# Combining the experts' rows: seven token groups in 128 slots, tokens beyond them sent aside through memory

## What is computed

```python
g_sel = argmax(g_logits)                    # one group of 8 for each token
top_val, top_idx = top_k(e_in_group, 2)     # two experts of that group
y[token] = sum over the two: gate * ((silu(x @ w1[e]) * (x @ w3[e])) @ w2[e])
h = h + y
out = rmsnorm(h, final_norm)
```

## Time and profile before

| | us |
|---|---|
| median of 3 timed runs | 1466.49 (1465.53 to 1470.39) |
| the profiled execution | 1461.49 |
| its span, first to last instruction | 1459.8 |
| experts, first up projection to last combine | 939.4 to 1448.6 |

### The profile page before, as it was taken

How to read it: one execution, slowest core, us unless ns; L and a number is a source line. 1 busy time by engine, 2 the same in 40 slices (tenths; PEclk the granted TensorE clock), 3 DMA queues, 4 the chain that set the end, 5 groups by cost and what they waited for, 6 DMA issues and landing times. The chain is left out here.

```text
span 1459.8 us, 22021 instructions
## 1 busy us (share of the span) xinstructions
PE 1420.7 (97%) x8759; PEld 1013.9 (69%) x8759; DVE 780.8 (53%) x1703; ACT 515.7 (35%) x992; POOL 82.4 (6%) x115
## 2 busy tenths in 40 slices
PE   9999999999999999999989999899999999999995
PEld 8888887797878877677768888755545555545552
DVE  6455565433531154667758555555654655555553
ACT  6525354222332147555543456412121212212121
POOL 0000000000000000000000011200101101011000
PEclk9999999999999999999999999999999999999998
DMA  6111111112224335112236634899999999999940
GB/s 176 44 30 44 30 38 36 30 33 87 86 88 118 104 92 161 59 37 73 72 122 221 252 123 151 307 411 418 419 420 419 420 418 419 419 418 419 419 199 16
DMA packets 114680, 286.38 MB, mean 196 GB/s; under 512 B 28926, under 2 KB 75006, under 8 KB 90258
## 3 DMA queue, kind: packets, MB, share of 16 engines
q1 hardware_dynamic: 105362, 263.95, 48.4%
q0 software_dynamic: 9216, 21.02, 3.7%
HBM read 270.19 MB, written 23.10 MB: 201 GB/s over the span
## 5 line engine op out<-in xcount | busy, mean ns | idle before, releaser
L134 PE MATMUL ps<-uTh,h_wh 128*128 128x512 f32 (+2 forms) x672 | 255.5, 380 | 0.0
L136 PE MATMUL ps<-uTh,h_wl 128*128 128x512 f32 (+2 forms) x672 | 247.8, 369 | 0.0
L135 PE MATMUL ps<-uTl,h_wh 128*128 128x512 f32 (+2 forms) x672 | 247.7, 369 | 0.0
L2617 PE MATMUL ps<-r,m_xT 128*64 128x256 f32 x2048 | 246.2, 391 | 0.4 <-DVE m_xT L2412 0.4
L2617 PEld LDWEIGHTS ps<-r,m_xT 128*64 128x64 f32 x2048 | 141.4, 134 | 89.3 <-issue 13.7
L134 PEld LDWEIGHTS ps<-uTh,h_wh 128*128 128x128 f32 x672 | 126.3, 188 | 22.5 <-issue 0.4
L136 PEld LDWEIGHTS ps<-uTh,h_wl 128*128 128x128 f32 x672 | 126.3, 188 | 18.9
L135 PEld LDWEIGHTS ps<-uTl,h_wh 128*128 128x128 f32 x672 | 126.5, 188 | 18.3 <-issue 0.2
L589 DVE TENSOR_TENSOR h_wl<-h_w,h_wh 128x1024 fp32r<-128x1024 f32 (+1 forms) x42 | 50.6, 1204 | 157.0 <-ACT h_wh L402 156.9
L2582 PE MATMUL ps<-r,m_small 128*64 128x512 f32 x512 | 124.1, 605 | 1.6 <-DVE m_small L2486 0.9
L2333 ACT ACTIVATE m_small<-ps,scale 128x128 f32<-128x128 f32 x64 | 23.4, 366 | 266.9 <-PE ps L2617 266.9
(11 more groups left out here) (423 smaller groups left out, 2356.8 us busy)
## 6 DMA issues: line engine op xcount, KB each, us to landing
r<-in_w SPq DMA_DIRECT2D x190, 1024.0 KB, 15.8
h_w<-in_w_in SPq DMA_DIRECT2D x37, 512.0 KB, 4.2
gates<-h_sg POOLq DMA_DIRECT2D x16, 512.0 KB, 2.9
br_gate<-gates SPq DMA_DIRECT2D x14, 512.0 KB, 4.9
e_wo<-in_w_out SPq DMA_DIRECT2D x4, 1024.0 KB, 7.9
f_x<-in_x SPq DMA_DIRECT2D x8, 512.0 KB, 5.0
h_half<-f_half SPq DMA_DIRECT2D x8, 512.0 KB
gates<-br_gate SPq DMA_DIRECT2D x6, 512.0 KB, 2.7
```

The source lines that it names most:

```text
L134: pe.matmul(out, lh, rh, start=start, stop=False)
L135: pe.matmul(out, lh, rl, start=False, stop=False)
L136: return pe.matmul(out, ll, rh, start=False, stop=stop)
L2617: ins = pe.matmul(up_out(e, 0, DE, CAP * f, CAP * (f + 1)).rearrange("p (r f) -> p r f", r=2), xT[i % 2][:, j, CAP * k:CAP * (k + 1)], g.r ...
```

## The change

1. For seven groups the token list kept on the chip is its first 128. `combine` leaves out line 2595 for the first EDGE = 28 pairs; the last group (pairs 28 to 31) keeps `rest`, now in another buffer. `roots`, `sums` and `scaled` handle `o2` for the last group alone, with one instruction of 128 x 512 in place of two and gains of its own (`gain_half`).
2. `one_hot` writes its matrix with a row sum (`found`): 1 if the slot's token is among the 128, else 0. A further instruction of one column makes `aside` = 2 token + choice, plus 4096 where it was found, which is out of bounds. It runs at the start of the next even iteration, ahead of the hidden rows. `spread_rows` and `row` move an iteration forward.
3. POOL sends each of the 28 pairs aside with an indirect scatter of its 128 rows to `g.y` at `aside`: only rows of tokens beyond the 128 move. The gather into the same buffer waits for that scatter's landing and for the last `low` of the pair, in place of `combine`.
4. At the start of the experts, `past`, `past_ranks`, `past_spots`, `past_list` and `past_lists` number the tokens beyond and make a list of them. During the last group two gathers fetch their two rows, DVE adds, ACT and DVE normalise, and a third indirect DMA writes them out.
5. `g.y` is filled beforehand, 8 DMAs of 1 MB from memory to memory, one after each of the weight loads J = 2..9 on SP. The slot lists carry a fourth column block (the choice), from which `dstf` is made.
6. The repeat through `late_blocks` is now taken if the tokens beyond, summed over seven groups, exceed 128, or the last group exceeds 192. `lo` is one buffer of 128 x 512.

```diff
...
             for J in range(2, len(JOBS)):
                 sp.wait_ge(wl_ok, J - 1)
                 load_w(J)
+                if J < 10:
+                    n = J - 2
+                    sp.dma_start(g.y[n * 256:(n + 1) * 256, :], g.x[0, n % 4 * 256:(n % 4 + 1) * 256, :]).then_inc(y_filled, 16)
...
+            dve.wait_ge(rows_ok, 6)
+            for k, part in halves:
+                dve.scalar_tensor_tensor(out=g.dstf[part, :], in0=srcf[part, :], scalar=2.0,
+                                         in1=LISTS(3 * EXPERTS, EXPERTS)[part, k::2], op0=ALU.mult, op1=ALU.add).then_inc(rows_ok, 1)
...
-                pe.matmul(LISTS(0, 3 * EXPERTS), Pm[:, 1, :], V[t % 2][:, 1, 0:3, :].rearrange("p v e -> p (v e)"),
+                pe.matmul(LISTS(0, 4 * EXPERTS), Pm[:, 1, :], V[t % 2][:, 1, :, :].rearrange("p v e -> p (v e)"),
...
             def give(n):
                 pool.wait_ge(to_ok, 3)
-                pool.wait_ge(o_ok, 3 * n + 1)
...
-                pool.wait_ge(o_ok, 3 * n + 3)
-                settle(pool, g)
-                pool.indirect_dma_start(out=g.out[0].rearrange("t (c d) -> (t c) d", c=2),
-                                        out_offset=bass.IndirectOffsetOnAxis(ap=to_half[:, n:n + 1], axis=0),
-                                        in_=o2[:, :], in_offset=None, bounds_check=2 * SEQ - 1, oob_is_err=False).then_inc(o2_out, 16)
...
-            pool.memset(x[ROWBUF - 1], 0.0).then_inc(rows_zero, 1)
-            for n in range(XB - 1, PAIRS):
-                if n == ROWBUF - 1:
-                    pool.wait_ge(rows_zero, 1)
-                elif n >= ROWBUF:
-                    pool.wait_ge(cmb_mm, 2 * (n - ROWBUF) + 2)
-                if n >= 2 * PER and n % PER == 0:
-                    give(n // PER - 2)
...
+            def gather(n):
...
+            for i in range(EDGE):
+                pool.wait_ge(aside_ok, i + 1)
+                pool.wait_ge(y_ok, 4 * i + 4)
+                settle(pool, g)
+                pool.indirect_dma_start(out=g.y, out_offset=bass.IndirectOffsetOnAxis(ap=aside[:, i:i + 1], axis=0),
+                                        in_=x[i % ROWBUF], in_offset=None,
+                                        bounds_check=2 * SEQ - 1, oob_is_err=False).then_inc(aside_out, 16)
+                if i and i % PER == 0:
+                    give(i // PER - 1)
+                pool.wait_ge(aside_out, 16 * i + 16)
+                pool.wait_ge(lo_ok, 2 * i + 2)
+                gather(i + ROWBUF)
+            pool.wait_ge(dn_mm, EXPERTS - PER_GROUP + 2)
+            pool.wait_ge(beyond_ok, 3)
+            for r in range(2):
+                settle(pool, g)
+                pool.indirect_dma_start(out=left_y[:, r, :], out_offset=None, in_=g.y,
+                                        in_offset=bass.IndirectOffsetOnAxis(ap=aside_at[:, r:r + 1], axis=0),
+                                        bounds_check=2 * SEQ - 1, oob_is_err=False).then_inc(left_in, 16)
             give(GROUPS - 2)
+            pool.wait_ge(left_ok, 1)
+            settle(pool, g)
+            pool.indirect_dma_start(out=g.out[0], out_offset=bass.IndirectOffsetOnAxis(ap=aside_at[:, 2:3], axis=0),
+                                    in_=left_y[:, 0, :], in_offset=None, bounds_check=SEQ - 1, oob_is_err=False).then_inc(left_out, 16)
             give(GROUPS - 1)
...
-                if n:
-                    act.wait_ge(o2_out, 16 * n)
-                act.activation(o2[:, :], bank(MORE_BANK), ACT.Square, accum_out=st[:, 0:1]).then_inc(ss_ok, 1)
-                act.wait_ge(s2_ok, 2 * n + 2)
-                act.wait_ge(ss_ok, 2 * n + 2)
+                if n == GROUPS - 1:
+                    act.activation(o2, bank(MORE_BANK), ACT.Square, accum_out=st[:, 0:1]).then_inc(ss_ok, 1)
+                    act.wait_ge(s2_ok, 2)
+                act.wait_ge(ss_ok, n + 1)
...
+            def left_root():
+                act.wait_ge(left_sum, 1)
+                act.activation(left_y[:, 1, :], left_y[:, 0, :], ACT.Square, accum_out=st[:, 1:2]).then_inc(left_ss, 1)
+                act.wait_ge(left_ss, 1)
+                act.activation(st[:, 1:2], st[:, 1:2], ACT.Sqrt, scale=1.0 / D, bias=g.eps[:, :]).then_inc(left_rt, 1)
+                act.activation(warm[:, :], g.eps[:, :], ACT.Sigmoid)
...
+            def past_spots():
+                dve.wait_ge(beyond_mm, 1)
+                c.link(dve.tensor_copy(beyond_at, beyond_out))
+                for t in range(TT):
+                    dve.tensor_scalar(beyond_spot[t], g.io_group[:, 0:P], beyond_at[:, t:t + 1], beyond[:, t:t + 1], ALU.is_equal,
+                                      ALU.mult).then_inc(beyond_spot_ok, 1)
...
+            def left_added():
+                dve.wait_ge(left_in, 32)
+                dve.tensor_tensor(left_y[:, 0, :], left_y[:, 0, :], left_y[:, 1, :], ALU.add).then_inc(left_sum, 1)
...
+            def left_scaled():
+                dve.wait_ge(left_rt, 1)
+                dve.reciprocal(st[:, 1:2], st[:, 1:2]).then_inc(left_rc, 1)
+                dve.wait_ge(left_rc, 1)
+                dve.scalar_tensor_tensor(out=left_y[:, 0, :], in0=left_y[:, 0, :], scalar=st[:, 1:2], in1=gain, op0=ALU.mult,
+                                         op1=ALU.mult).then_inc(left_ok, 1)
...
             def one_hot(i):
                 dve.wait_ge(row_mm, i // PER + 1)
                 if i >= 2:
                     dve.wait_ge(cmb_mm, 2 * i - 2)
-                dve.tensor_scalar(hot[i % 2], row_out[:, 0:P], g.srcf[:, i:i + 1], None, ALU.is_equal).then_inc(hot_ok, 1)
-                dve.tensor_scalar(rest(i % 2, 64, 64), row_out[:, P:GC], g.srcf[:, i:i + 1], None, ALU.is_equal).then_inc(hot_ok, 1)
-
-            def sums(n):
-                dve.wait_ge(ss_ok, 2 * n + 2)
+                dve.scalar_tensor_tensor(out=hot[i % 2], in0=row_out[:, 0:P], scalar=g.srcf[:, i:i + 1], in1=g.ones[:, :],
+                                         op0=ALU.is_equal, op1=ALU.mult, accum_out=found[:, i % 2:i % 2 + 1]).then_inc(hot_ok, 1)
+                if i < EDGE:
+                    dve.wait_ge(hot_ok, hot_at(i))
+                    dve.scalar_tensor_tensor(out=aside[:, i:i + 1], in0=found[:, i % 2:i % 2 + 1], scalar=SKIP, in1=g.dstf[:, i:i + 1],
+                                             op0=ALU.mult, op1=ALU.add).then_inc(aside_ok, 1)
+                else:
+                    if i == EDGE:
+                        for b in range(3):
+                            dve.tensor_scalar(rest(b, 0, 64), g.ones[:, 0:64], 0.0, None, ALU.mult).then_inc(hot_ok, 1)
+                    dve.tensor_scalar(rest(i % 2, 64, 64), row_out[:, P:GC], g.srcf[:, i:i + 1], None, ALU.is_equal).then_inc(hot_ok, 1)
+
...
-                for q in range(2):
-                    rows = slice(64 * q, 64 * (q + 1))
-                    dve.scalar_tensor_tensor(out=o2[rows, :], in0=bank(MORE_BANK, 0, 512, 64 * q, 64 * (q + 1)), scalar=st[rows, 7:8],
-                                             in1=gain[rows, 512 * q:512 * (q + 1)], op0=ALU.mult, op1=ALU.mult).then_inc(o_ok, 1)
+                if n == GROUPS - 1:
+                    dve.wait_ge(gain_half_in, 32)
+                    dve.scalar_tensor_tensor(out=o2, in0=bank(MORE_BANK), scalar=st[:, 7:8], in1=gain_half, op0=ALU.mult,
+                                             op1=ALU.mult).then_inc(o_ok, 1)
...
-            for b in range(3):
-                dve.tensor_scalar(rest(b, 0, 64), g.ones[:, 0:64], 0.0, None, ALU.mult).then_inc(hot_ok, 1)
+            dve.tensor_scalar(st, g.ones[:, 0:8], 1.0, None, ALU.mult).then_inc(st_ok, 1)
...
+                if e % 2 == 0 and 4 <= e < EXPERTS - 2:
+                    one_hot(e // 2 - 1)
...
+                    past()
...
-                if e % PER_GROUP == 1:
-                    spread_rows(e // PER_GROUP)
+                    spread_rows(0)
+                if e == 2:
+                    past_spots()
                 if e % 2 == 0 and 2 <= e < EXPERTS - 2:
                     low(e // 2 - 1, 0)
-                    one_hot(e // 2 - 1)
-                if e % PER_GROUP == 1 and e > PER_GROUP:
-                    sums(e // PER_GROUP - 1)
+                if e == 2:
+                    one_hot(0)
+                if e == 3:
+                    past_lists()
+                if e % PER_GROUP == 0 and e:
+                    spread_rows(e // PER_GROUP)
+                if e == EXPERTS - 4:
+                    left_added()
+                if e == EXPERTS - 3:
+                    left_scaled()
...
+            def past_ranks():
+                pe.wait_ge(member_ok, 4)
+                pe.matmul(beyond_out, g.upper[:, :], beyond, start=True, stop=False)
+                for n in range(1, TT):
+                    ins = pe.matmul(beyond_out[:, n:TT], g.ones[:, :], beyond[:, 0:TT - n], start=False, stop=n == TT - 1)
+                ins.then_inc(beyond_mm, 1)
+
+            def past_list():
+                pe.wait_ge(beyond_spot_ok, TT)
```

(47 more changed lines are left out.)

85 lines of the change are left out of this document (61 added, 24 removed).

## The result

The changed kernel takes 1444.85 us (1440.82 to 1445.83, four runs) where the kernel before took 1466.01 (1461.87 to 1470.39, four runs on the same chip): a ratio of 0.985, 95% interval 0.9815 to 0.9885, a gain of 21.2 us. Forecast were 24 us and 1442.5. The profiled execution of after took 1445.61 us, its span is 1443.9.

The account below looks back on a forecast made before the run. PE was taken to set the pace, with DMA a second bound. PE's side, 26.3 + 9.9 - 4.5 = 31.7 us, is capped by DMA at 24.7; less up to 1, gain 24: 1466.5 - 24 = 1442.5 us, range 1434 to 1453.

Parts of the forecast that it names:

- The likeliest case: Whole kernel: PE gives up 31.7 us, DMA allows 24.7, the smaller counts; gain 21 to 27 us, chance 0.58.
- (a): Combines of the first 28 pairs: 112 places lose PE matmuls at 0.235 us each, saving 26.3 us.
- part is given back: Rival: second combines wait for `high` and `low`, so 13.2 us are lost; 1448, or 1455 with DVE's instructions; chance 0.18.
- (b): Turn of each group: PE's waits for one-hots (8.5 us) and transposed rows (1.4) go, saving 9.9 us.
- (c): Start of the experts: new `past_ranks` (1.9 us) and `past_list` (2.6) matmuls cost PE 4.5 us.
- (d): POOL's scatter, wait and gather: 11.3 us a pair against PE's 14.3, landing taken as 9.3; it fits, cost 0.
- The rival needed 13.2 us: Rival: POOL becomes the bound from scatter landings of 13.2 us; at 14 us 26 us slower, 1492; chance 0.08.
- (e): Weight loads on full DMA engines: the last pieces' landing lets PE gain at most 24.7 us, spread 22 to 27.
- The ceiling by the Trainium skill: Weight transfers at 435 instead of 419 GB/s would be 16 us shorter, letting all 31.7 us come; not adopted.
- Time to landing: Sign in the weight loads: landing time grows by 7 us a group instead of 2.3, to over 40.
- PE's clock falls when it waits: Rival in the last two groups: waits for weights lower PE's clock, costing 0 to 3 us, within the forecast's range.
- (f): The rest: `g.y` fills 0, last group's gathers and pieces 0 to 1 us, nothing from the second scatter's issue.

Follow-up runs that it names:

- after_again: The changed kernel itself measured once more, nothing altered: 1446.74 us, ratio 0.9865 to the kernel before.
- turn_only: Kernel before without squaring, joining sums, scaling and scattering of `o2` for seven groups, all matmuls kept: 1456.58 us, ratio 0.9927.
- two_scatters: Changed kernel with every scatter aside issued and awaited twice: 1529.69 us, ratio 1.042 to the kernel before.
- short_past: Changed kernel with 2 instead of 8 matmuls in each of `past_ranks` and `past_list`: 1443.66 us, ratio 0.9843 to the kernel before.
- mm_only: Kernel before with only the matmuls of line 2595 left out for the first 28 pairs: 1442.53 us, ratio 0.9834.
- light_after: Changed kernel with half of each down-projection weight load left out from expert 8 on: 1433.57 us, ratio 0.9783 to the kernel before.
- no_scatter: Changed kernel without the 28 scatters aside and the wait for their landing: 1442.12 us, ratio 0.9827 to the kernel before.
- less_mm: Changed kernel without the lower-part matmul for the first 28 pairs (56 matmuls): 1445.95 us, ratio 0.9856 to the kernel before.
- fill_before: Kernel before with only the eight fills of `g.y` added: 1469.74 us, ratio 1.001.

## Why the prediction was right, and where its sizes were off

The likeliest case came true: PE gives up more than DMA allows, and the smaller number is the gain. 21.2 us were gained (21.3 in after_again) where 24 were forecast, at the lower edge of the 21 to 27 that the forecast allowed.

- **(a), the matmuls: right.** 26.3 forecast, 25.1 measured alone. The ends of a combine in after, to be held against the earlier trace rows:

```profile
1290.54 0.39 PE L2715 MATMUL ps<-m_lo,m_hot 128*128 128x512 f32 x1
1290.86 1.94 PE L2704 MATMUL ps<-r,m_small 128*64 128x512 f32 x8
```

`down` follows 0.32 us after the lower part's matmul, and line 2717 keeps 16 instructions. The rival "part is given back" fell: alone, the matmuls bring about all of their gain (22 to 27 us by the interval).
- **(b), the turn: right.** 9.9 forecast; measured alone 11.0 by the medians, with an interval of 8.5 to 12.9, and 7.8 in the experts' part. Moving the one-hots was not needed for it: turn_only has them in their old place and no such wait.
- **(c), the start: a quarter too much.** `past_ranks` takes 1.8 us (1.9 forecast). `past_list` takes 1.8, not 2.6: the earlier trace rows, from which 0.32 a matmul was taken, show 8 columns with two matmuls between other work, while eight of one column in a row start 0.23 apart.

```profile
964.24 1.70 PE L2662 MATMUL ps<-m_gain,ones 128*128 128x7 f32 x14
...
973.54 1.95 PE L2668 MATMUL ps<-tok,m_o 128*128 128x1 f32 x16
```

- **(d), POOL: right.** The scatters land after 7.6 us, where 9.3 was assumed; no matmul waits for gathered rows.

```profile
DMA to landing us min/median/max: 6.3/7.6/8.6
```

The rival needed 13.2 us; two_scatters, with 16.0 for the two, shows that it is real and priced about right. The Trainium skill's fit of 2.0 us plus bytes ("DMA: Bandwidth & Descriptors", section "Anatomy of one DMA — SWDGE (gpsimd) path"), weighed in the prediction, would have put the landing at a quarter of what it is; the row of the half-full gathers, 8.0, was the better guide.
- **(e), the ceiling: right in kind, 3 to 4 us too generous.** The step that was mis-sized is its drift. *The place*: the forecast looked at the last pieces of e = 63. What held PE last is e = 61, whose weights are complete at 1400.26 in after, 456.3 from the mark. In before they were 6.8 us ahead of that: 939.4 + 456.3 - 6.8 = 1388.9. (Read directly, they were issued at 1364.9, and loads of that stretch land 23.8 to 24.6 us later.) With the up projection at 1415.4 that is a reserve of 26.5. The last pieces gave 24.7 with 2.4 of drift taken off, which is 27.1, so the place hardly matters. *The drift of the weights*, forecast 2.4 us (1.4 of traffic, 1 of idling), is 6.8 by +450. Of it 4.2 arise in the first 100 us, where 1 had been put down for idling: over 960 to 1000 DMA moves 378 instead of 410 GB/s, 40 x 32 / 418 = 3.1 us. 1.3 to 1.7 of the 4.2 are the `past` matmuls (short_past), about 1 is within the spread of the reading; the rest, 1.5 to 2 us, was not tracked down, and mm_only has some of it. The other 2.6 come while the engines are full, 2.2 of them by the scatters, where I had counted their bytes and nothing for rows that don't move. *Together*: 26.5 - 6.8 = 19.7 us at e = 61, and 0.8 more behind it, make the 20.5 of the two profiles.
- **The ceiling by the Trainium skill**, 435 GB/s ("DMA: Bandwidth & Descriptors", section "Where 436 GB/s comes from"), would have let all of PE's gain through. The same section puts the limit of transfers between HBM and SBUF at about 358 GB/s, which the prediction left out, and these loads are such transfers. Neither is what was measured: DMA stays at 417 to 418 in every full slice of after, and light_after shows the 11 us that this costs.
- **Time to landing: right at first, "over 40 us" wrong.** In after_again, by groups from 960 on (stretches as in the earlier trace rows), the weight loads land after 12.1, 19.1 and 28.0 us (medians), a growth of 7 and 9 a group where 7 was forecast. Then it stops: 28.9, 29.2, 28.6, and 28.9 (26.9 to 31.6) in 1335 to 1384. The backlog went on, but SP couldn't issue it. Its instructions for a load, least, median and most duration in ns, first before, then after:

```profile
L1534 SPq DMA_DIRECT2D r<-in_w x10: 327/380/434, 1340.6 to 1372.3; - x10
```

```profile
L1538 SPq DMA_DIRECT2D r<-in_w x12: 432/2168/6807, 1337.1 to 1379.0; - x12
```

From 0.4 us an issue grew to 2.2, up to 6.8: some 29 us of transfers at 418 GB/s, 12 MB, stand in the queue, and the next issue seems to wait for room. PE's waits begin with the seventh group (e = 48, at 1294), where "about the sixth group on" was said; they are 0.9 us on average and up to 2.0, where under 1 was said. The last data was to land at about 1411; in after DMA is full until about 1412 and falls empty at about 1418; 4.6 of the 7 us between are the later start.
- **PE's clock falls when it waits: at times, and worth 0 to 1.6 us.** The rival said 0 to 3. In after the clock fell once, to 0.72 over 1335 to 1340, behind a wait of 2.02 us; in short_past once behind 2.09, in no_scatter once behind 1.73. The up projection then takes 5.44 us instead of 3.84. But it isn't the length of the wait alone: less_mm kept the clock in full behind its longest, and after_again behind 2.41.

```profile
1272.36 3.85 PE L2739 MATMUL ps<-r,m_xT 128*64 128x256 f32 x32 [2.90 <-DMA r<-in_w]
```

Such a fall is absorbed where PE waits again afterwards, as the rival held, and shows at the last wait, which it didn't see.
- **The fill and the second scatter at the end (f)**: nothing, as said (fill_before, and the last two scatters are issued at 1436.90 and 1438.17).

## What to carry to other kernels

When two resources are both full, the one that is waited for sets the time, and the growth of the other's time to landing gives its distance: 2.3 us of growth in each group, less the reserve of filled buffers, gave the ceiling, to 3 or 4 us, before the change was built. A gain on the first is cut off at that ceiling, and from there small costs of the second count, those of scattered rows that don't move and of a few microseconds in which its engines idle among them. To learn which bound holds, take away work on one side only: 13 us less of PE's work bought nothing here, and 29 MB less of loads bought 11 us.

## What the runs showed of the hardware beyond that

- An indirect scatter of 128 rows with nearly all indices out of bounds is not nearly free: it lands after 7.6 us beside full engines and takes some 0.1 us of all 16 of them, about 0.07 of it beyond its bytes (both estimates from after and no_scatter), and brings some 141 packets under 512 B.
- A full queue shows on the issuing engine: a load's issue on SP takes 0.4 us while there is room and 2.2 us (up to 6.8) with some 29 us of transfers ahead, and from then on the time to landing stays at 28 to 29 us and no longer shows the backlog.
- In two profiled executions of one and the same kernel, after and after_again, the first up projection starts 4.9 us apart (944.0 and 939.1), and 3 us of it are there at the first projection already (21.0 and 17.9); the part behind it differs by 0.4. A difference of a few us between two profiles is best taken from a mark within the program.
